# Two fused transformer-style blocks on one core: the RG-LRU branch of the first block projected before HGRN2, and both recurrences moved into other projections

## The reference, cut to what matters

```python
hn = rmsnorm(h, e_norm)
u = hn @ e_w_in                       # 2048 x 6144: q, f, v, z of HGRN2; x, z of RG-LRU, 1024 each
ya = hgrn2(q, f, v, lb)               # S_t = diag(f_t) S_{t-1} + (1-f_t) i_t^T, 8 heads of 128
ya = head_rmsnorm(ya) * silu(za)
xc = causal_conv(xb, b_conv_w, b_conv_b)          # 4 taps
r, ig = sigmoid(xc @ w_r + b_r), sigmoid(xc @ w_i + b_i)   # 8 blocks of 128
a = exp(-8 r softplus(-lam)); hs = scan(a, sqrt(1 - a*a) * ig * xc)
yb = hs * silu(zb)
h = h + concat(ya, yb) @ e_w_out      # 2048 x 2048
pl = rmsnorm(p @ ple_w);  h = h + sigmoid(h @ ple_gate_w) * pl
```

## Time and profile before

| what | value |
|---|---|
| median of 3 runs | 3710.47 us (3709.07 to 3712.82) |
| the profiled execution's own time | 3708.12 us |
| its span | 3706.3 us |
| busy share of the span: PE / PE weight load / DVE / ACT | 95% / 81% / 57% / 46% |
| mean granted TensorE clock | 0.982 of full speed |
| HBM read over the span | 623.88 MB, 169 GB/s with what is written |

### The profile page before, as it was taken

One profiled execution on the slowest core, in us unless ns is written; L12 is line 12 of the kernel. 1 busy time (PEld: TensorE's weight loads), 2 busy tenths in 40 slices (PEclk: granted clock), 3 DMA queues, 4 the chain that ended last, 5 costly groups with the idle time before them and its releaser, 6 DMA issues.

```text
span 3706.3 us, 43338 instructions
## 1 busy us (share of the span) xinstructions
PE 3527.0 (95%) x18526; PEld 3004.3 (81%) x18526; DVE 2114.4 (57%) x2180; ACT 1703.5 (46%) x1977; POOL 18.8 (1%) x34
## 2 busy tenths in 40 slices
PE   7997899999899998988999999999999799999999
PEld 6886778878777887877888888888888688888887
DVE  5467656644556766555555555567655555555454
ACT  5433454345544556444443434454745444344343
POOL 0000000000000000000000000000000000000000
PEclk9998999999999999999999999999999999999999
DMA  6544455554455433443555555554434355555554
GB/s 215 193 144 140 140 171 179 177 177 161 146 195 188 162 137 129 156 169 105 192 193 189 186 193 193 188 179 166 137 127 158 114 182 187 193 188 193 193 184 168
DMA packets 88240, 628.78 MB, mean 170 GB/s; under 512 B 9984, under 2 KB 10224, under 8 KB 13168
## 3 DMA queue, kind: packets, MB, share of 16 engines
q1 hardware_dynamic: 85104, 611.75, 48.7%
q0 software_dynamic: 2944, 14.26, 1.1%
HBM read 623.88 MB, written 2.10 MB: 169 GB/s over the span
## 4 chain that ended last, share of the span: by engine, by line
PE 85%; DVE 8%; ACT 4%; DMA 1%; issue 1%; DVEq 0%; POOL 0%; ACTq 0%; POOLq 0%
PE G L536 25%; PE G L528 13%; PE G L530 13%; PE G L529 13%; PE G L538 12%; DVE w_lo L447 3%; ACT w_hi L439 2%; PE M L796 1%; PE G L520 1%; PE G L521 1%; PE G L522 1%; PE M L1123 1%; PE M L1170 1%; PE M L1038 0%; DMA w_raw<-in_s_ssd 0%
## 5 line engine op out<-in xcount | busy, mean ns | idle before, releaser
L447 DVE TENSOR_TENSOR w_lo<-w_raw,w_hi 128x2048 fp32r<-128x2048 f32 (+1 forms) x585 | 1328.7, 2272 | 1338.2 <-ACT w_hi L439 1337.8
L439 ACT ACTIVATE w_hi<-w_raw 128x2048 fp32r<-128x2048 f32 (+1 forms) x585 | 1110.8, 1899 | 1723.8 <-PE G L538 826.7
L536 PE MATMUL G<-x_halves,w_hi 128*128 128x512 f32 x4256 | 1348.4, 398 | 26.4 <-DVE w_lo L447 14.7
L538 PEld LDWEIGHTS G<-x_halves,w_lo 128*128 128x128 f32 x4256 | 802.1, 188 | 188.9
L538 PE MATMUL G<-x_halves,w_lo 128*128 128x256 f32 x4256 | 841.9, 279 | 0.0
L528 PE MATMUL G<-w_hi,y_halves 128*128 128x512 f32 x1776 | 702.7, 396 | 40.1 <-DMA arena<-in_b_w_i 14.4
L530 PE MATMUL G<-w_hi,y_halves 128*128 128x512 f32 x1776 | 694.8, 391 | 0.0
L529 PE MATMUL G<-w_lo,y_halves 128*128 128x512 f32 x1776 | 694.7, 391 | 0.0
L536 PEld LDWEIGHTS G<-x_halves,w_hi 128*128 128x128 f32 x4256 | 652.1, 189 | 30.9 <-issue 14.7
L528 PEld LDWEIGHTS G<-w_hi,y_halves 128*128 128x128 f32 x1776 | 335.8, 189 | 112.7 <-issue 17.5
L530 PEld LDWEIGHTS G<-w_hi,y_halves 128*128 128x128 f32 x1776 | 335.5, 189 | 70.7
(11 more groups left out here) (410 smaller groups left out, 2547.2 us busy)
## 6 DMA issues: line engine op xcount, KB each, us to landing
w_raw<-in_s_up SPq DMA_DIRECT2D x176, 1024.0 KB, 4.9
w_raw<-in_s_down SPq DMA_DIRECT2D x88, 1024.0 KB, 4.9
w_raw<-in_s_ssd SPq DMA_DIRECT2D x40, 1024.0 KB, 4.9
w_raw<-in_s_hgrn SPq DMA_DIRECT2D x32, 1024.0 KB, 4.9
w_raw<-in_s_gate SPq DMA_DIRECT2D x32, 1024.0 KB, 4.8
w_raw<-in_s_mlstm SPq DMA_DIRECT2D x32, 1024.0 KB, 4.8
w_raw<-in_s_mlstm_gate SPq DMA_DIRECT2D x32, 1024.0 KB, 4.9
w_raw<-in_s_lru SPq DMA_DIRECT2D x16, 1024.0 KB, 4.9
```

What stands on the lines that cost most here:

```text
L439: act.activation(whi[p % SETS][:, 0:n_], raw[p % RAW][:, 0:n_], ACT.Copy).then_inc(S("hi_ready"), 1)
L447: dve.tensor_tensor(wlo[p % SETS][:, 0:n_], raw[p % RAW][:, 0:n_], whi[p % SETS][:, 0:n_].bitcast(F32), ALU.subtract).then_inc(S("lo_ready ...
L536: pe.matmul(o, hi[:, k, f], x2, start=first, stop=False, skip_group_check=True)
L538: mm = pe.matmul(o[:, 0:T], lo[:, k, f], x2[:, 0:T], start=False, stop=last, skip_group_check=True)
```

## The change

RG-LRU is projected first. Its x part is now of the kind "conv" (taps inside the evacuation, from two small pads), its z part stays in `res[:, 1]` until it is used. The order becomes `lru` (pieces 0 to 15), `hgrn` (16 to 47), `e_out_b` (48 to 55), `e_out_a` (56 to 63). RG-LRU's gates, activations and scan hang on pieces 10 to 20, HGRN2's levels on pieces 34 to 47, its norm and transposes on 49 to 53, its preparation on DVE on 33. Both handovers of the layer are gone; a few waits on semaphores (`fm_acted`, `set_free`, `lru_a`) stand in their place. POOL issues the gate weights after piece 3 has ended, the reload of x after `lru_lo`, and the gain of the next norm after the second piece of `e_out_a`.

```diff
-    names = ["hgrn", "lru_scan", "ml_heads"]
+    names = ["ml_heads"]
...
+    s["lru"] = deep("e_w_in", 0, 4096, 2048)
     s["hgrn"] = deep("e_w_in", 0, 0, 2048) + wide("e_w_in", 0, 2048, 2048)
-    s["lru"] = deep("e_w_in", 0, 4096, 2048)
+    s["e_out_b"] = wide("e_w_out", 0, 0, D, 8, 8)
     s["e_out_a"] = wide("e_w_out", 0, 0, D, 0, 8)
-    s["e_out_b"] = wide("e_w_out", 0, 0, D, 8, 8)
...
-        plan("lru", *[("fm", "x", 0, "fmul", (None, early_xp, j)) for j in range(4)],
-             *[("fm", "x", 0, "fmul", (ACT.Silu, early_zb, j)) for j in range(4)])
+        plan("lru", *[("fm", "x", 0, "conv", (lr["xc"], lr["pad"], "b_conv_w", "b_conv_b", j)) for j in range(4)],
+             *[("fm", "x", 0, "fmul", (ACT.Silu, lr_zb, j)) for j in range(4)])
...
-        for name in ("hgrn", "ssd0"):
+        for name in ("lru", "ssd0"):
             for c in plans[name][0:2]:
                 c.late = 4
...
+            plans["e_out_b"][0].need = {0: ("lru_lo", 1)}
...
-        HGRN_STEPS = (0, 2, 4, 5, 7, 9, 11, 12, 13, 14, 15)
-        LRU_STEPS = (1, 3, 5)
+        HGRN_STEPS = (18, 20, 22, 24, 26, 27, 29, 31, 33, 34, 37)
...
+        def hgrn_at(eng, program):
+            for p in HGRN_STEPS:
+                at_piece(eng, first_piece["hgrn"] + p, lambda: next(program, None))
...
+            at_piece(pe, 10, lambda: gate(0))
+            at_piece(pe, 12, lambda: gate(1))
...
+            for p, step in ((10, lambda: gate(0)), (12, lambda: gate(1)), (13, tanh), (14, decay), (16, root), (20, high)):
+                at_piece(act, p, step)
...
         def hgrn_dve(dve):
             q, f, k, attn = (hg[x] for x in ("q", "f", "k", "attn"))
+            dve.wait_ge(S("fm_acted"), 12)
...
+            for p, step in ((15, gated), (17, scan), (19, out), (20, low)):
+                at_piece(dve, p, step)
...
-            pool.wait_ge(S("phase_done"), PH["lru_scan"])
+            pool.wait_ge(S("piece_done"), started("lru", 3))
...
-            pool.wait_ge(S("res_left"), 1)
+            pool.wait_ge(S("lru_lo"), 1)
             load(res[:], dram["x"].rearrange("b (t p) d -> p (b t) d", p=P), "res_back")
 
-            pool.wait_ge(S("lru_lo"), 1)
+            pool.wait_ge(S("piece_done"), started("e_out_a", 1))
...
-            pe_gemm(pe, "hgrn", {3: [lambda: row_pe(pe)]}, xt=True)
+            lru_pe(pe)
+            pe_gemm(pe, "lru", {3: [lambda: row_pe(pe)]}, xt=True)
             pe.wait_ge(S("const"), CONSTS)
-            handover(pe, "hgrn")
-            pe_gemm(pe, "lru", between(hgrn_pe(pe), HGRN_STEPS))
-            handover(pe, "lru_scan")
-            ready(pe)
-            pe_gemm(pe, "e_out_a", between(lru_pe(pe), LRU_STEPS))
-            pe.wait_ge(S("lru_lo"), 1)
             base = []
-            pe_gemm(pe, "e_out_b", turns_pe(pe, "e_out_b", base))
+            hgrn_at(pe, hgrn_pe(pe, base))
+            pe_gemm(pe, "hgrn")
+            pe_gemm(pe, "e_out_b")
+            laid, base = base[0], []
+            pe_gemm(pe, "e_out_a", turns_pe(pe, "e_out_a", base), laid)
...
+            lru_dve(dve)
+            dve_gemm(dve, "lru", {2: [stats], 3: [lambda: row_dve(dve)], 6: [prep]})
+            program = hgrn_dve(dve)
+            at_piece(dve, first_piece["hgrn"] + 17, lambda: next(program))
+            hgrn_at(dve, program)
+            dve_gemm(dve, "hgrn")
             ple_p_dve(dve)
-            feed = between(lru_dve(dve), LRU_STEPS)
-
-            feed[0] = [lambda: dve.wait_ge(S("res_back"), 16)]
-            dve_gemm(dve, "e_out_a", feed)
-            dve_gemm(dve, "e_out_b", turns(2, dve_fm, dve, KT, halves["x"], 0))
+            dve_gemm(dve, "e_out_b", {0: [lambda: dve.wait_ge(S("res_back"), 16)]})
+            dve_gemm(dve, "e_out_a", turns(2, dve_fm, dve, KT, halves["x"], 0))
```

More of the change, by code:

```diff
@@ L604, in finish @@
                             act.activation(hg["k"][:, 2 * j:2 * j + 2, :], o, ACT.Sigmoid, scale=-1.0)
-                            act.activation(o, o, ACT.Sigmoid)
+                            ins = act.activation(o, o, ACT.Sigmoid)
                         else:
-                            act.activation(o, o, fn)
+                            ins = act.activation(o, o, fn)
+                        ins.then_inc(S("fm_acted"), 1)
                     at_piece(act, after, finish)
@@ L1133, in hgrn_pe @@
             pe.wait_ge(S("hg_attn"), n(pe, "hg_attn"))
+            for c in plans["hgrn"][8:10]:
+                pe.wait_ge(S(f"set_free{c.slot}"), c.c // 2 + 1)
             for t in range(NT):
@@ L1146, in lru_pe, with gate @@
         def lru_pe(pe):
[L1147 to L1152, removed]
+            def gate(g):
+                if g == 0:
+                    ready(pe)
+                    pe.wait_ge(S("gate_w"), 32)
+                    pe.wait_ge(S("conv_done"), plans["lru"][3].k)
+                else:
+                    pe.wait_ge(S("lru_sig"), 1)
                 for b in range(8):
@@ L1385, in hgrn_act @@
         def hgrn_act(act):
-            for _ in range(10):
+            for _ in range(9):
                 yield
@@ L1400, in lru_act, with gate @@
         def lru_act(act):
[L1401 to L1405, removed]
+            def gate(g):
+                dst, bias = ((lr["r"], "b_b_r"), (lr["i"], "b_b_i"))[g]
+                act.wait_ge(S("lru_gate"), g + 1)
                 for b in range(8):
@@ L1411, in lru_act, with tanh, decay, root @@
                     act.drain().then_inc(S("lru_sig"), 1)
[L1412 to L1424, removed]
+            def tanh():
+                for b in range(8):
+                    ins = act.activation(lr["th"][:, b, :], lr["r"][:, b, :], ACT.Tanh, scale=c8[:, b:b + 1])
+                link(act, ins)
+            def decay():
+                for b in range(8):
+                    ins = act.activation(lr["r"][:, b, :], lr["r"][:, b, :], ACT.Exp, scale=nc8[:, b:b + 1])
+                ins.then_inc(S("lru_a"), 1)
+            def root():
+                act.wait_ge(S("lru_m2"), 1)
+                act.activation(lr["th"], lr["th"], ACT.Sqrt).then_inc(S("lru_m"), 1)
+            def high():
+                act.wait_ge(S("lru_y"), 1)
+                act.activation(yh[:, 8:16, :], lr["i"], ACT.Copy).then_inc(S("lru_hi"), 1)
+            for p, step in ((10, lambda: gate(0)), (12, lambda: gate(1)), (13, tanh), (14, decay), (16, root), (20, high)):
+                at_piece(act, p, step)
         def ple_p_act(act):
@@ L1713, in hgrn_dve @@
             y, sq = flat(q), flat(k)
+            for c in plans["hgrn"][10:12]:
+                dve.wait_ge(S(f"set_free{c.slot}"), c.c // 2 + 1)
             link(dve, dve.tensor_tensor(sq, y, y, ALU.mult))
@@ L1725, in lru_dve @@
         def lru_dve(dve):
[L1726 to L1734, removed]
@@ L1745, in lru_dve @@
[L1745 to L1754, removed]
@@ new lines, in scan, with out @@
+            def scan():
+                dve.wait_ge(S("lru_m"), 1)
+                link(dve, dve.tensor_tensor(i_, i_, th, ALU.mult))
+                for b in range(8):
+                    ins = dve.tensor_tensor_scan(hs[:, b, :], a_[:, b, :], i_[:, b, :], 0.0, ALU.mult, ALU.add)
+                link(dve, ins)
+            def out():
+                dve.wait_ge(S("fm_acted"), 4)
+                link(dve, dve.tensor_tensor(i_, hs, lr_zb, ALU.mult))
+                dve.drain().then_inc(S("lru_y"), 1)
@@ L1757, in ple_p_dve, with low @@
+            def low():
+                dve.wait_ge(S("lru_hi"), 1)
+                dve.tensor_tensor(yl[:, 8:16, :], i_, yh[:, 8:16, :].bitcast(F32), ALU.subtract).then_inc(S("lru_lo"), 1)
+            for p, step in ((15, gated), (17, scan), (19, out), (20, low)):
+                at_piece(dve, p, step)
         def ple_p_dve(dve):
@@ L2235, in prep @@
                 prep_act(act)
[L2237 to L2240, removed]
+            lru_act(act)
+            act_gemm(act, "lru", {2: [squares], 3: [lambda: n(act, "fm_full")], 6: [prep]})
+            hgrn_at(act, hgrn_act(act))
+            act_gemm(act, "hgrn")
             ple_p_act(act)
-            act_gemm(act, "e_out_a", between(lru_act(act), LRU_STEPS))
-            act_gemm(act, "e_out_b", turns(2, act_fm, act, KT, halves["x"], 0))
+            act_gemm(act, "e_out_b")
+            act_gemm(act, "e_out_a", turns(2, act_fm, act, KT, halves["x"], 0))
             act_gemm(act, "ple0", tail_act(act, halves["x"], None, None, 0, 1))
```

40 lines of the change are left out of this document (17 added, 23 removed).

## The result

The changed kernel took 3681.25 us (median of 4 runs, 3676.41 to 3683.92) against 3711.3 of the kernel before on the same chip (4 runs): a ratio of 0.9919, with a 95% interval of 0.9907 to 0.9931. It is faster by some 0.8%. The forecast was 3684. On another chip it took 3678.02 (5 runs) against 3708.55 (9 runs), a ratio of 0.9915 [0.9901, 0.9928].

A forecast was written before the change was run, and what follows sets the result against it. PE is busy 95% of the span, so only its standstills can be won: 48.2 - 6.6 - 6.9 - 0.4 - 8.3 = 26.0 us off the 3710.47 median gives 3684.5, written 3684; range 3662 to 3697.

The forecast's parts named there:

- What goes (48.2): Before gate0: handover 6.2, norm, transposes, second handover and gate-weight load 24.4, output waits 17.6; sum 48.2 us gone.
- the 14.4: PE's old wait for the RG-LRU gate weights, 14.4 us, taken as counted from the load's issue; early issue makes it nothing.
- The 17.6 of the output: Output: waits of 3.9 for a weight half and 9.6 for lru_lo, slow pieces 2.0 and 2.1; 17.6 us gone.
- p10 (loss 6.6): RG-LRU piece 10: conv taps and constants' preparation on DVE delay its start from 85.3 to 91.9, loss 6.6 us.
- p12 to p20 (loss 7.3): Pieces 12 to 20: evacuation behind gated products, wait 5.1 before piece 18, 6.9 with slow piece; scan step adds 0.4.
- the load before tanh: ACT's function-set load of 1.28 us, counted with tanh as 3.3 us in the chain leading to the wait before piece 18.
- x (0): POOL's 2 MB reload of x beside the weight stream: taken as 0, with 2.2 us kept for the range.
- Level 0 (loss 8.3): First HGRN2 level, after piece 34: DVE's preparation late, wait 7.0 and slow piece 2.0 against 0.7 before; loss 8.3 us.
- All is covered: Rival, 12%: none of the three new waits reaches PE, so the full 48.2 us is won, giving 3662.
- ACT's backlog is longer: Rival, 12%: five set switches before piece 18 each cost another 1.28 us, chunk 7's sum 6.4 later, giving 3691.
- Waits only moved: Rival, 2%: output b takes the norm's wait, level 0 and piece 18 double; result within 7 us of now.
- The slower outcome: Rival, 2%: moved vector work, 62.6 us at pieces 4 to 20, is uncovered, giving 3733; needs over 40 reaching PE.

The follow-up runs named there:

- the late issue: Changed kernel with POOL issuing the two gate-weight loads only after piece 10 has ended, instead of piece 3: 3698.5 us, gate0 18.2 us later.
- the second profile: The changed kernel once more, unedited, on another chip: 3678.02 us (5 runs), gate0 at 468.46 us.
- the three cures: Changed kernel with level preparation earlier, RG-LRU's vector steps later, constants' preparation later and split, and the attn memset at piece 28: 3654.92 us.

## Why the prediction was right

**What goes (48.2).** All of these waits are gone from the list of the changed kernel. Two were put back and returned at about their size: a handover cost 6.2 by my working and 7.1 at another piece; the norm's wait was 6.4 and came back as 6.5. For the gate weights the late issue shows that the load needs its cover. It does not confirm the 14.4, which the prediction reads as a wait from the issue: 4.5 of it lay before the issue, at the handover, and the 15.1 are loads that took longer beside the stream. The 17.6 of the output were not put back.

**p10 (loss 6.6).** Forecast to start at 91.9; it started at 92.28, with p4 1.65 later than before, and at 91.03 in the second profile, with p4 at 44.08. The chain was as told: DVE at 86.83 with the last small product, ACT's sines at 87.1, the high half at 87.41, the low half at 89.34, the sum at 91.55. The slow piece cost 1.9 instead of the 2.8 that I had left equal. The hit to 0.4 us is partly luck: the working starts from the old trace's times, and counted from p4 the loss was 5.3 in the first profile and 5.9 in the second, not 6.6; the late p4 made up the rest.

**p12 to p20 (loss 7.3).** It was 5.9: p17 to p20 took 28.22 instead of 4 x 5.57. The wait before p18 was 3.6, not 5.1. The step that was off is the load before tanh, 1.28, which does not occur. The slow piece was not a term of its own either. In the second profile p18 ran at the full clock, in 5.68, and PE waited 1.8 before p20 for the sum after the scan; in the first p18 took 7.24 and that wait was 0.3. The four pieces take 28.2 both times: since DVE was late before p20 too, the slow p18 cost nothing.

**x (0).** It landed 10.6 us after its issue, against 8.8, and no wait of PE stands beside it. The stream did feel it: the weight piece issued 1.9 us behind it took 9.0 us to land instead of 4.9 and came 0.3 us after x. That is close to the case in which a piece waits for all of it, and the cover hid it. With the three cures it no longer did.

**Level 0 (loss 8.3).** Wait 7.0 as forecast, and 1.8 for the clock instead of 2.0. The norm was ready at 390.4, 12.1 after PE's products, and the transposes at 394.8 didn't wait: forecast 12 and three pieces.

**The sum.** Gate0 starts 29.8 earlier, where I had 26.0. Of the 3.8, 0.9 is p10's slow piece, 1.4 p17 to p20, and 0.2 level 0, while p10's start was 0.4 worse. That leaves 1.7. The waits of levels 1 to 7, of which the prediction says "it stays", fell from 1.1 to 0.5, which gives 0.6, and the transposes lengthen the way from p53 to p54 by 1.7 where I had 2.0, which gives 0.3. Some 0.8 us stay open. The gain of the whole was 25.5 for the pair of profiles, and 30.1 and 30.5 between the medians on the two chips. That the pair comes so close to 26.0 is luck: 3.8 more were won up to gate0, and 4.3 were lost behind it, of which the working says nothing. Against the medians the gain was forecast some 4 too small.

**The rivals.** "All is covered" fell with the three waits, and the run with the cures shows what it would have been worth: 3654.92, which is 23.1 less than the changed kernel beside it. It is 53.6 less than the kernel before, more than the 48.2, since the cures also end the wait of 6.1 before p10 that the old order had. "ACT's backlog is longer" needed twice the 1.28 us for each load; the run with three more loads excludes it. "Waits only moved" is excluded by the result, and the handover put back shows one wait that did not move. The slower outcome needed over 40 us of vector work to reach PE; from p4 to p20 about 10 more than before did, waits and clock together (5.3 up to p10, counted from p4, and 5.9 at p17 to p20, less 0.9 for the faster p10).

## What to carry to other kernels

When work of other engines is hung into a weight stream, write down for each step when the tensor engine ends the piece, when the next half or evacuation is wanted, and what stands ahead of it in the queue; here that gave each new wait within 1.5 us. A long step ahead of an evacuation costs its excess over the cover, and moving it by one piece, or cutting it in two, wins that back: three such edits of a few lines were worth 23 us, beside the 30 of the reordering. A wait removed is won only if the work that it had hidden gets another place, so look for that work before the order is changed.

## What the runs showed of the hardware

- The same two 512 KB loads of POOL were done 9.7 us after the first issue with the stream nearly at rest (362.09 + 4.7 - 357.11), and 14.3 beside it. Of the 4.6 between them, 2.8 lie between the two issues (5.0 against 7.8) and 1.8 in the second landing (4.7 against 6.5). In the changed kernel, beside the stream at another place, it was 13.9, with 6.9 between the issues and 7.0 for the second landing. What sets the time between the issues no run shows.
- A 1 MB piece of the stream that SP issued 1.9 to 2.6 us behind POOL's 2 MB reload of x landed after 9.0 us in the changed kernel, and after 8.6, 9.3 and 9.6 in the runs with the preparation moved, with the RG-LRU steps moved and with all cures, where such pieces mostly take 4.9. Each came 0.3 to 0.6 us after x itself.
- ACT takes up the next activation 0.01 to 0.02 us after a table load, in five of the six loads from 105 to 136 us (the sixth waited for PE) and in the three added ones; silu to tanh needs no load.
- After a wait of 3.6 us the granted clock of the next piece was 0.76 in one profile of the changed kernel and 1.00 in the other; after the 4.4 of the restored handover it was 0.66. The same wait of 7.0 was followed by a first level at 0.68 in one run and at 0.54 in another, worth 1.2 us. So a difference of 1 or 2 us at such a place proves nothing about an edit elsewhere.
